# A hybrid decoder layer: a shorter routing chain, and an out-projection transposed by two engines

## What is computed

```python
h = h + jnp.concatenate([o_att, o_ssm], axis=-1) @ w_out[l]
h = h + hier_moe(rms_norm(h, ffn_norm_w[l]), router_g_w[l], ...)

def hier_moe(u, rg_w, rg_b, re_w, re_b, w_gate, w_up, w_down):
    g_prob = softmax(t @ rg_w + rg_b)          # 4 groups
    g_p, g_idx = lax.top_k(g_prob, 1)
    e_logit = (t @ re_w + re_b) ...            # the 4 experts of that group
    e_l, e_idx = lax.top_k(e_logit, 2)
    w = softmax(e_l) * g_p
    ... out = sum of w * (silu(t @ w_gate) * (t @ w_up)) @ w_down over both experts
```

## Time and profile before

| | us |
|---|---|
| three runs, median (lowest to highest) | 1240.83 (1238.91 to 1256.93) |
| the profiled execution | 1238.48 |
| its span, first to last instruction | 1236.7 |
| busy: TensorE, VectorE, ScalarE, GpSimd | 1135.4, 721.7, 290.9, 118.9 |
| mean granted TensorE clock, of 1 | 0.954 |

### The profile page before, as it was taken

The page is one execution under the profiler, slowest core; times in us unless marked ns, Lnnn a source line. Parts: engine busy times, 40 slices in busy tenths (PEclk is TensorE's granted clock), DMA queues, the critical chain, the costliest instruction groups (busy, mean ns, idle before and its releaser), DMA issues. The chain is left out here.

```text
span 1236.7 us, 14771 instructions
## 1 busy us (share of the span) xinstructions
PE 1135.4 (92%) x4847; PEld 687.0 (56%) x4848; DVE 721.7 (58%) x1642; ACT 290.9 (24%) x707; POOL 118.9 (10%) x175
## 2 busy tenths in 40 slices
PE   6999999999999999999999797899962999999996
PEld 3444654445477777777777686355542444444442
DVE  2422213333036676776666397588747878888883
ACT  2311221111234443343433245311100000000000
POOL 0000000000000000000000070000000233333332
PEclk9999999999969999999999998899975999999998
DMA  6110520200000000000000300622154967999532
GB/s 241 55 39 1 152 69 1 68 0 16 1 2 3 4 3 2 2 2 2 2 1 1 128 9 1 216 103 88 66 195 152 332 232 259 323 383 349 188 106 78
DMA packets 72065, 119.78 MB, mean 97 GB/s; under 512 B 14304, under 2 KB 49216, under 8 KB 72008
## 3 DMA queue, kind: packets, MB, share of 16 engines
q1 hardware_dynamic: 60920, 88.08, 21.0%
q0 software_dynamic: 11088, 30.95, 7.1%
HBM read 105.90 MB, written 21.50 MB: 103 GB/s over the span
## 5 line engine op out<-in xcount | busy, mean ns | idle before, releaser
L1367 DVE STREAM_TRANSPOSE big_w<-big_w 32x256 f32<-32x256 f32 x416 | 181.3, 436 | 35.8 <-DMA big_w<-hn_dram,misc 26.1
L458 PE MATMUL ps<-big_w,big_u 128*128 128x512 f32 (+1 forms) x512 | 201.4, 548 | 0.0
L1910 PE MATMUL ps<-ring_gate_up,big_w 128*128 x400 | 181.4, 597 | 14.4 <-DVE big_w L1367 14.4
L458 PEld LDWEIGHTS ps<-big_w,big_u 128*128 128x128 f32 x512 | 95.7, 191 | 90.4 <-issue 84.2
L948 PE MATMUL ps<-ring_down,big_u 128*128 128x65 f32 x912 | 119.1, 280 | 18.6 <-ACT big_u L1000 9.5
L991 ACT ACTIVATE big_u<-ps,big_w 128x384 f32<-128x384 f32 (+15 forms) x192 | 90.0, 522 | 187.6 <-DVE big_w L1043 169.2
L1910 PEld LDWEIGHTS ps<-ring_gate_up,big_w 128*128 128x128 f32 x400 | 74.6, 192 | 99.5 <-issue 99.5
L948 PEld LDWEIGHTS ps<-ring_down,big_u 128*128 128x128 f32 x912 | 110.6, 195 | 34.0 <-ACT big_u L1000 16.7
L917 PE MATMUL ps<-ring_down,misc 97*128 97x512 f32 (+3 forms) x320 | 125.3, 503 | 0.0
L1043 DVE TENSOR_REDUCE big_w<-ps 128x2 f32<-128x768 f32 (+15 forms) x96 | 78.1, 814 | 64.5 <-PE ps L922 42.3
L1505 PE MATMUL ps<-big_w,big_u 128*128 128x512 f32 x256 | 114.9, 604 | 0.9 <-DVE big_u L1590 0.9
(11 more groups left out here) (286 smaller groups left out, 1150.9 us busy)
## 6 DMA issues: line engine op xcount, KB each, us to landing
ring_gate_up<-in_w_gate SPq DMA_DIRECT2D x16, 1024.0 KB, 9.2
ring_gate_up<-in_w_up SPq DMA_DIRECT2D x16, 1024.0 KB, 12.8
ring_down<-in_w_down SPq DMA_DIRECT2D x16, 1024.0 KB, 14.8
big_w<-in_w_in SPq DMA_DIRECT2D x10, 1024.0 KB, 7.4
misc<-in_x SPq DMA_DIRECT2D x16, 512.0 KB, 3.4
big_w<-in_w_out SPq DMA_DIRECT2D x8, 512.0 KB, 6.6
hn_dram<-big_u SPq DMA_DIRECT2D x8, 512.0 KB, 2.6
out<-ring_gate_up SPq DMA_DIRECT2D x8, 512.0 KB, 3.6
```

The source lines that it names most:

```text
L458: last = nc.tensor.matmul(ps[:, b, 0:width], uT[:, k, c * P:(c + 1) * P], wbuf[:, n % 2, k, 0:width], start=(k == 0), stop=(k == KD - 1))
L1367: last = nc.vector.transpose(dst[j * 32:(j + 1) * 32, :, i * 32:(i + 1) * 32], src[i * 32:(i + 1) * 32, :, j * 32:(j + 1) * 32])
L1910: last = nc.tensor.matmul(ps[:, 2 + b, :], xT[:, b, k, :], ring_gu[:, bass.ds(at + k * 2 * D_EXP, BANK)], start=(k == 0), stop=(k == KD - 1))
```

## The change

1. **Out-projection.** Chunks 1 to 7: the attention half of `catT` is transposed by TensorE (four transposes into PSUM bank 0) and copied by ScalarE; VectorE transposes only the SSD half. Chunk 0 stays as it was.
2. **Logits without the norm.** TensorE transposes `h` instead of `hn`, in two halves of four, the first within its own chunk; ScalarE copies both out (VectorE the very last). The norm weight is multiplied into the router weights once, 1/rms into the logits afterwards. `hn` is still written and stored.
3. **Choice in two parts.** `choose` runs for chunks 0 to 5 during chunk 7 and for chunks 6 and 7 at the end, with 3 short steps in place of a full ranking of the groups. Counts and running sums come from bf16 products that accumulate in one bank. Places within slots are found for chunks 0 to 5 early.
4. **Tables.** Tokens first, in bf16 with two parts (32 products), weights later, in bf16 with three parts (16 products). The first slot's index is written by VectorE, and its gather goes out before the weights are formed.
5. **Experts in the same block.** `experts` returns its five programs, which follow on each engine's list without the meeting of all engines; they wait for a semaphore `places_ready`. The first slot's rows are transposed by TensorE (8 transposes) and copied by ScalarE, not by VectorE.

```diff
+            def attention_transposes(c):
+                pe.wait_ge(cat_ready, 3 * c + 1)
+                if c >= 2:
+                    pe.wait_ge(att_transposed, c - 1)
+                for k in range(4):
+                    last = nc.tensor.transpose(ps[:, 0, k * P:(k + 1) * P], o_att[:, c, k * P:(k + 1) * P], ident[:, :])
+                last.then_inc(att_full, 1)
...
             for c in range(NT):
-                project_out(c)
...
+                out_products(c, 0, 0, 4)
+                if c >= 1:
+                    h_transposes(c - 1, 1)
+                if c + 1 < NT:
+                    attention_transposes(c + 1)
+                out_products(c, 0, 4, KD)
...
+                out_products(c, 1, 0, 4)
+                if c >= 1:
+                    route(c - 1)
+                if c == NT - 1:
+                    count_early()
+                out_products(c, 1, 4, 6)
+                h_transposes(c, 0)
+                out_products(c, 1, 6, KD)
+            h_transposes(NT - 1, 1)
             route(NT - 1)
...
+            count_rest()
...
             for c in range(NT):
+                if c >= 1:
+                    evacuate_hT(c - 1, 1)
+                if c + 1 < NT:
+                    copy_attention(c + 1)
                 if c + 2 < NT:
                     scale_cat(c + 2)
+                evacuate_hT(c, 0)
                 h_stats(c)
...
+            dve.wait_ge(tok_out, 1)
+            o.done(nc.vector.tensor_copy(up_tile, ps[:, 6, 256 + TABLE:256 + 2 * TABLE]))
+            o.done(tt(up, ps[:, 6, 256:256 + TABLE], up_tile, ALU.add))
+            ts(M["tok_idx"][:, 0:1], up[:, 0:1], -1.0, 0.0, ALU.add, ALU.max).then_inc(M["idx_ready"], 1)
...
+        pe.wait_ge(s_rows[0], 16)
+        for k in range(KD):
+            last = nc.tensor.transpose(ps[:, 4 + k // 4, (k % 4) * P:(k % 4 + 1) * P], xg[:, 0, k * P:(k + 1) * P], ident[:, :])
+            if k % 4 == 3:
+                last.then_inc(first_x_full, 1)
+        pe.wait_ge(first_x, 2)
+        pe.wait_ge(places_ready, 1)
+        last_slot = over_slots(pe, step)
```

More of the change, by code:

```diff
@@ L12 @@
+from collections import namedtuple
 from contextlib import ExitStack
@@ L159, in done, with build @@
         self.wait()
-def build(nc, A, C, out, last="experts"):
+def build(nc, A, C, out, last="merge"):
     stack = ExitStack()
@@ L1497, in first_cat_transposes @@
                         last.then_inc(cat_full, 1)
[L1499 to L1506, removed]
-                    last.then_inc(o_full, 1)
[L1508 to L1511, removed]
@@ new lines, in out_products, with h_transposes @@
+            def out_products(c, half, k0, k1):
+                for k in range(k0, k1):
+                    last = nc.tensor.matmul(ps[:, 2 + half, :], catT[:, c % 2, k, :],
+                                            w_out[:, k, half * BANK:(half + 1) * BANK], start=(k == 0), stop=(k == KD - 1))
+                if k1 == KD:
+                    last.then_inc(o_full, 1)
+            def h_transposes(c, j):
+                pe.wait_ge(h_ready, 2 * c + j + 1)
+                if c >= 1:
+                    pe.wait_ge(hT_evac[j], c)
+                for k in range(4 * j, 4 * j + 4):
+                    last = nc.tensor.transpose(ps[:, 4 + j, (k % 4) * P:(k % 4 + 1) * P],
+                                               h[:, c, k * P:(k + 1) * P], ident[:, :])
+                last.then_inc(hT_full[j], 1)
@@ new lines, in count_rest @@
+            def count_rest():
+                pe.wait_ge(counts_in, 2)
+                for c in range(EARLY, NT):
+                    left = NT - c
+                    last = nc.tensor.matmul(ps[:, 7, (c + 1) * N_EXP:(NT + 1) * N_EXP], onesb,
+                                            both[:, c * N_EXP:(c + 1) * N_EXP].unsqueeze(1).broadcast_to([P, left, N_EXP]),
+                                            start=False, stop=True, skip_group_check=True)
+                nc.tensor.matmul(ps[:, 7, EARLY * N_EXP:NT * N_EXP], trib, both[:, EARLY * N_EXP:NT * N_EXP],
+                                 start=False, stop=True, skip_group_check=True).then_inc(counts_out, 1)
@@ L1532, in _ @@
             for c in range(NT):
-                project_out(c)
+                pe.wait_ge(cat_transposed, c + 1)
                 if c >= 1:
-                    hn_transposes(c - 1)
-            route(NT - 2)
-            hn_transposes(NT - 1)
-            route(NT - 1)
[L1540 to L1543, removed]
@@ new lines, in _ @@
+                if c >= 1:
+                    route(c - 1)
[5 more added lines that the diff above has]
+            h_transposes(NT - 1, 1)
+            route(NT - 1)
+            count_rest()
+            pe.wait_ge(tok_in, 1)
+            for v in range(2):
+                for i in range(2 * NT):
+                    if v == 1 and i == 0:
+                        pe.wait_ge(tok_in, 2)
+                    last = nc.tensor.matmul(ps[:, 6, 256 + v * TABLE:256 + (v + 1) * TABLE], place_hot[:, i // NT, i % NT, :],
+                                            tokens[:, v, i, :], start=(i == 0), stop=(i == 2 * NT - 1))
@@ L1645, in rank @@
[L1645 to L1652, removed]
@@ L1661, in _ @@
[L1661 to L1668 removed]
+                if c == NT - 2:
+                    choose(0, EARLY)
```

731 lines of the change are left out of this document (407 added, 324 removed).

## The result

The changed kernel takes 1240.39 us (median of 20 executions, 1228.31 to 1246.59). The kernel before, run in turn with it on the same chip, takes 1251.14 us (20 executions, 1238.60 to 1257.33). The ratio is 0.992, with a 95% interval of 0.9893 to 0.9948: the change gains some 10 us. It is less than 2%, and it is there. But the time is not the 1228 us of the forecast, and it lies above the forecast's range.

The account below looks back on a forecast made before the run. TensorE was taken as the bound, with a 50.3 us near-stop before the experts that the change shortens to 30.7: 19.6 us gained, 6.7 given back, 12.9 net; 1238.5 - 12.9 = 1225.6, plus 2.35, said as 1228, range 1222 to 1235.

Parts of the forecast that it names:

- The last step: Whole kernel: profiled 1238.5 us less 12.9 gives 1225.6; adding 2.35 for the median of runs gives 1227.9, said as 1228.
- Ahead of T: Up to T, the end of the last out-projection product: added transposes 4.4, a route 1.8, counts 0.5; T 6.7 us later.
- The seven early counts: Out-projection: seven bf16 products for early expert counts, at 0.06 to 0.07 us each, 0.5 us (0.2 to 1.5).
- The choice: After the last out-projection product (T): choosing experts for two chunks starts at T + 3.8, 20 operations taking 3.9 us.
- The gather's issue: Gather of the first slot's rows, issued at T + 18.4, T being the end of the last out-projection product.
- The end of the gap: First expert product at T + 30.7, counted from the last out-projection product's end; gap shrinks from 50.3 us, 19.6 gained.
- Experts: Expert loop: loads of experts 3 and 4 have less lead over the first product, 2.7 us, which costs nothing.
- a sign of being wrong: The forecast is wrong if the expert loop, 277.5 us long, changes its length.
- The gather did not go at the loads' pace: Rival: first slot's gather takes the weight loads' pace, 17.4 us at most, leaving 2.6 us gain, 1238 us; chance 0.06.
- Short work among products: Rival: 40 interleaved transposes cost 0.28 us each, making the last out-projection product 6.7 us later, 1234.6 us; chance 0.11.
- The clock was not up at the first expert product: Rival: transposes and table products raise the clock, so the first ten expert instructions take 1.6 us less, 1226; chance 0.07.
- It did not fall inside the out-projection: Rival: clock drops to 1.2 GHz in the out-projection; one chunk gives 1245 us, two 1262; chance 0.04.

Follow-up runs that it names:

- b_warm: The kernel before plus 32 idle bf16 products, two ahead of each of the first 16 score steps of attend; 1237.18 us, ratio 0.9894.
- b_again: The kernel before, run once more unchanged; 1251.35 us over 12 executions, ratio 1.0008.
- a_again: The changed kernel, run once more unchanged; 1241.56 us over 12 executions, ratio 0.9926 to the kernel before.
- b_warm2: The same kernel as b_warm, run again in another group; 1236.39 us over 6 executions, ratio 0.9884 to the kernel before.
- a_only_warm: The changed kernel plus the same 32 idle products early in attend and nothing else; 1227.84 us, ratio 0.9814 to the kernel before.
- after: The changed kernel in its first profiled execution, which took 1239.13 us; the kernel's median is 1240.39 us, ratio 0.992 to the kernel before.
- a_fill: The changed kernel with expert 1 announced before SyncE waits for the plan, plus 68 idle products between last out-projection and first expert product; 1233.66 us, ratio 0.9876.
- a_late_load: The changed kernel with expert 1 announced before SyncE waits for the plan, and expert 2's loads issued after the plan; 1227.61 us, ratio 0.9844.

## Why the prediction was right or wrong

**The level: the step that failed.** The last step took the profiled execution's own time less 12.9 us and added 2.35 us to come to the median of three runs. Both anchors were low, by the luck of the draw: 20 executions of the same kernel have a median of 1251.14, 12.7 us above that profile. Taken from there, the same gain gives 1251.1 - 12.9 = 1238.2, against 1240.39 measured. The range was built only from what the change could do; that executions of the kernel before differ by 18 us (1238.91 to 1256.93, with the median 2 above the lowest and 16 below the highest) stood in the table ahead of the prediction and entered neither end. The low clock that makes them differ stood in its trace too (37.6 us), in stages that the change doesn't touch, and the prediction gave it no term; how much it varies could be seen only over executions. b_warm shows the cause.

**Ahead of T: 6.7 forecast, 6.0 measured**, 5.3 and 5.1 in the pairs b_again and a_again, b_warm2 and a_only_warm. The period was to be 17.0 and is 16.84. The transposes cost what the row said: 0.43 us for four in a row amid products, 0.109 each. The seven early counts took 0.2 us, not 0.5. The Trainium skill's 275 ns for a transpose ("TensorE: Matmul & The Clock Gate", Part 4) is not what this kernel pays.

**The choice, T + 3.8 forecast,** stood at T + 3.8; its 20 operations took 3.9 us, as summed. The starts and places ended at T + 13.2 (13.8), the second token operand at T + 14.2 (15.2), where the bf16 TENSOR_SCALAR of 512 columns took 0.35 us and not 0.7; the bf16 TENSOR_TENSOR took 0.69, no less than in fp32. The gather's issue: T + 17.2 (18.4). The gather took 7.4 us (6.9) and landed at T + 24.6 (25.3); the eight transposes lasted 1.97 us, as at 1.2 GHz.

**The end of the gap: T + 30.7 forecast, T + 30.2 measured.** Two misses cancel in part. The chain ahead of TensorE's way into the experts ended at T + 27.2 with ScalarE's second copy, not at 28.0 with VectorE's places, which stood at T + 26.3. From the end of that copy (954.81) to the first product (957.81) it took 3.0 us, not 2.7. The 3.63 us of idle time in the row of TensorE hold 0.6 us of that copy as well. ScalarE in order of time, then TensorE's register loads:

```profile
954.21 0.60 ACT L1597 ACTIVATE big_w<-ps 128x512 f32<-128x512 f32 x1 [0.26 <-PE ps L1565]
...
L1422 PEldq TENSOR_LOAD <-misc x1: 503/503/503, 954.8 to 954.8; - x1
...
L1521 PEldq SEQ_ASSERT  x3: 18/18/18, 956.3 to 957.6; - x3
```

**Experts: "costs nothing" forecast, 2.0 to 3.4 us measured.** The step asked whether the weights would land in time, and they do. It did not ask what stands behind their issue on SyncE's list: two issues of 6.41 and 4.44 us, and behind them the word for expert 1. That wait is 1.8 to 3.3 us in after, a_again and a_only_warm. In a_only_warm the first 16 instructions took 10.10 us besides, against 8.80 in after. Removing the block boundary moved these issues to the moment at which TensorE wants that word. The forecast had named a change of this stage's length as a sign of being wrong, and so it was.

**The rivals.** The gather did not go at the loads' pace. Its chain does end last, at T + 27.2, but only 0.9 us behind the places: bringing it 3 us forward moved the gap by 0.7. Short work among products is not dear, by the period. The clock was not up at the first expert product, and where it had been raised earlier, in a_fill, it fell again in the 3.7 us of TensorE's way in. It did not fall inside the out-projection, with twelve transposes and a route in each 16.84 us: 1.00 from 821 to 911 us. The Trainium skill's rule that transposes don't count as activity for the clock (same title and part) would have worked against that; at this share of transposes nothing of it is seen.

**The sum.** 12.9 us forecast for the stages of the change, 11.2 to 12.1 measured (12.1 in the first two profiles, 11.2 in both later pairs): the mechanism and the gain were right, the level under it was not. That the sum comes so near is partly luck: 0.7 us ahead of T and 0.5 us in the gap were better than forecast, and the experts gave up the 2 to 3 us that had no term. That it stays within 2% was right.

## What to carry to other kernels

Before a gain is subtracted from a time, ask how that time stands in the kernel's spread: compare stages of two profiles rather than their ends, and look at the granted clock of stages that the change leaves alone. When work is moved past DMA issues, ask what the issuing engine says to others behind them, not only whether the data lands in time. A stretch in which TensorE does short work at 1.2 GHz may be worth more than the serial chain under study: 32 idle products gained as much here as a whole rewritten stage.

## What the runs showed of the hardware

- Added products shortened the kernel: 32 idle ones early in `attend` took 14 us off the kernel before and the standard deviation over executions from 5.7 to about 2 us.
- From one execution to the next of the same kernel the time rose by 0.35 to 0.38 us with each us more at 1.2 GHz.
- In the gap, 68 products held the granted clock at 1.00 through the eight transposes behind them; within the 3.74 us without work that followed it fell to 0.50.
- Issuing a 1 MB load on SyncE took 0.37 us for the first and up to 6.41 us for the fifth in a row.
- A gather of 128 rows took 7.4 us beside loads at 364 GB/s, and 4.4 us or less where those were fewer (117 GB/s):

```profile
944.00:952.00 8.00, 1.46 (x16) 1.25 (x16) 7.24 (x31) 0.34 (x1) 3.59 (x3) 0.50 1.08 364
```

```profile
938.00:944.00 6.00, 3.08 (x24) 2.82 (x24) 5.47 (x21) 0.46 (x1) 3.55 (x3) 0.50 0.39 117
```

The first stretch is of after, the second of a_late_load, each around its gather.
